# A hybrid scan kernel in which the SSD decay rows are loaded with repetition, head pairs share TensorE by column halves, and z is gated at its projection

## The chip, the cores and the metric

One core of one Trainium2 chip runs the whole program. The metric is the device time of one execution in microseconds. The engines are TensorE (PE in the rows), VectorE (DVE), ScalarE (ACT), GpSimd (POOL) and the queue processor SyncE (SP), which here only issues DMAs; ScalarE issues some too.

## The reference, cut to what matters

The model has two layers over 512 latent tokens and 256 context tokens (T = 768 columns in all), width 1024. The first layer runs a gated linear attention (GLA, 4 heads) and a Mamba-2 scan (SSD, 16 heads of 64 features, 2 groups with a state of 128) in both directions. The change is in the SSD part:

```python
dt = softplus(dt.reshape(b, l, 2, SSD_HEADS) + dt_bias)
log_a = dt * (-exp(a_log))
...
y, ss_f, ss_b = bidir_scan(ch, bh * dt[0], bh * dt[1], xh, log_a[0], log_a[1], init[2], init[3])
y = y + xh * d_skip
y = y.reshape(b, l, SSD_INNER) * silu(z)
y = rmsnorm(y.reshape(b, l, SSD_GROUPS, SSD_INNER // SSD_GROUPS), ssd_norm)
```

`bidir_scan` runs S_t = a_t S_(t-1) + k_t x_t, o_t = S_t q_t forwards and backwards. As matrices it is this: with g the running sum of log_a of a head, token s reaches token t by (B_s . C_t) dt_s exp(g_t - g_s), forwards for s <= t and backwards for s >= t, and the latent tokens also see the states at the end of the context. The rest of layer 1 (an mLSTM) and the two feed-forward blocks are not touched.

## The kernel before

**Layout.** Features lie on partitions, the 768 tokens are columns. Dense projections go unit by unit: a unit is 128 output features, its 8 weight blocks come through a ring of four, GpSimd splits them into a high and a low part (L600 to L603), and TensorE makes three products of each (L746, L820 for the mixed stage). `proj` in DRAM holds the 44 tiles of the input projection: x tiles from 32, z tiles from 24, B at 40 and 41, C at 42 and 43.

**Around the scan.** The mixed stage interleaves the units of g, z and x (table MIXED, L54) with the GLA heads; ScalarE evicts a unit's PSUM into `stage` (L1386). Then `out0` projects the GLA output to the residual (8 units, VectorE adds them at L2094). In its middle VectorE and ScalarE run the **row chain**: 32 rows, 16 heads in two directions. ScalarE loads `rowc` and `dcol` (L1487 to L1491), takes `r_ab` (L1494), VectorE softplus and the running sums `Grow` (L2122 to L2145) and `r_nb` (ln dt - g, L2148); TensorE turns `r_nb`, `r_al` into columns (L976, L979), copied to `nb` and `al` (L1516).

**The scan.** Eight pairs of heads. Per group of 8 heads `group_products` (L994 to L1001) makes B C of every chunk, `group_copies` (L1528) puts it into `cb` (six chunks of 128 tokens: four latent of 512 columns, two of context, 2560 columns) and B transposed into `Btok`. Per pair: TensorE transposes x (L1011), ScalarE copies it to `xtok` (L1532), VectorE weights it (`xal`, L2186), TensorE makes the context states (L1019), VectorE copies them (`ssS`, L2193). Per head:

- `rows` (L1030): TensorE spreads the head's row of g over 128 partitions by a one-hot product into PSUM, one slot of two banks for each direction.
- `exponents` (L2161): VectorE adds the column `nb` to the diagonal blocks; GpSimd sets the wrong side of them to -1e30 (L622, L626).
- `decays`: ScalarE takes the exponential of the strips off the diagonal straight from PSUM with `nb` as bias (L1549), of the first 512 columns into `Cb` (L1552), and of the masked diagonal blocks (L1556).
- `head_weights`: VectorE adds the backward diagonal blocks to the forward ones (L2171, L2173), multiplies all by `cb` into `Mm` (2560 columns, L2176), and C into `Cb` (L2178).
- `head_products`: four products of x with the weights (L1044), two of the states with `Cb` (L1046), two for the context (L1048), all into 64 of 128 partitions of one PSUM slot.

Then `output` adds D x (L2198) and multiplies by silu(z) (L2200), for which `gate_z` (L1560) loads its own table on ScalarE between two `decays`. x and z of a pair are loaded by ScalarE (L1503, L1504). At the end come squares, sums over features (L692), the spread of the norm (L698) and `out1`, the second output projection (L746).

**Order.** Each engine works its list in the order written and waits on counters; nothing is reordered. `Dm`, `Cb`, `xt`, `xtok`, `ssS` have two buffers.

## Time and profile before

| | |
|---|---|
| median of 3 runs | 2860.43 us (2858.86 to 2861.58) |
| profiled execution | 2862.67 us, span in the trace 2860.9 us |
| TensorE busy | 2559.3 us, 89% |
| VectorE busy | 1496.9 us, 52% |
| GpSimd busy | 1019.1 us, 36% |
| ScalarE busy | 644.4 us, 23% |
| granted TensorE clock, mean | 0.92 of full speed |
| the scan: end of `out0` to first product of `out1` | 676.8 to 993.7 us |

### The profile page before, as it was taken

How to read it: one execution, taken by the hardware profiler on the slowest of the kernel's cores; microseconds unless marked ns; L12 is line 12 of the kernel's file. 1: busy time of each engine (PE TensorE's matmuls, PEld its weight loads, DVE VectorE, ACT ScalarE, POOL GpSimd, SP SyncE). 2: the span in 40 equal slices, each digit the busy share in tenths (PEclk: the TensorE clock that was granted, in tenths of full speed). 3: DMA queues.
4: the chain of work that ended last, by engine and by line, in shares of the span. 5: the costliest groups of instructions: out<-in, count | busy, mean ns of one | idle time of the engine just before them, and what ended most of it. 6: DMA issues, size and time to landing. Idle time of an engine off the chain costs nothing.

```text
span 2860.9 us, 33680 instructions
## 1 busy us (share of the span) xinstructions
PE 2559.3 (89%) x12095; PEld 1946.5 (68%) x12095; DVE 1496.9 (52%) x2513; ACT 644.4 (23%) x984; POOL 1019.1 (36%) x806
## 2 busy tenths in 40 slices
PE   6999999968777799999999989699787796899998
PEld 2888888855333377888888878575444543788886
DVE  3685766654545535887788645520544345422223
ACT  3103444323444313100000032111222021210001
POOL 2443333322111042545434435333200310677663
PEclk9999999977777799999999989899888898999999
DMA  7753233421000021444434425445412210233331
GB/s 244 239 153 116 89 109 111 168 74 52 22 33 22 0 67 45 118 111 125 117 102 112 104 60 155 150 134 170 135 38 66 88 41 30 74 103 97 94 93 55
DMA packets 387698, 280.22 MB, mean 98 GB/s; under 512 B 31042, under 2 KB 350972, under 8 KB 387580
## 3 DMA queue, kind: packets, MB, share of 16 engines
q1 hardware_dynamic: 326876, 182.63, 22.2%
q10 hardware_dynamic: 60704, 96.00, 9.8%
q8 instruction: 76, 1.25, 0.2%
q14 instruction: 42, 0.34, 0.0%
HBM read 236.91 MB, written 41.68 MB: 97 GB/s over the span
## 4 chain that ended last, share of the span: by engine, by line
PE 80%; DVE 11%; ACT 5%; issue 2%; DMA 1%; ACTq 0%; SPq 0%; DVEq 0%; POOL 0%; POOLq 0%
PE PS L746 51%; PE PS L820 6%; PE PS L1222 3%; PE PS L1044 3%; PE PS L1030 2%; PE PS L1192 2%; PE PS L1129 1%; PE PS L910 1%; PE PS L677 1%; PE PS L1046 1%; PE PS L692 1%; ACT Dm L1549 1%; DVE Gn L1989 1%; PE PS L698 1%; PE PS L876 1%
## 5 line engine op out<-in xcount | busy, mean ns | idle before, releaser
L746 PE MATMUL PS<-act_hi,w_hi 128*128 128x512 f32 (+1 forms) x2080 | 639.1, 365 | 46.2 <-DVE act_lo L1911 18.1
L600 POOL TENSOR_TENSOR w_hi<-w_raw,ones 128x128 fp32r<-128x128 f32 x244 | 148.6, 609 | 1361.6 <-PE PS L746 855.2
L746 PE MATMUL PS<-act_lo,w_hi 128*128 128x512 f32 (+1 forms) x2080 | 623.9, 358 | 0.0
L746 PE MATMUL PS<-act_hi,w_lo 128*128 128x512 f32 (+1 forms) x2080 | 623.4, 357 | 0.0
L603 POOL TENSOR_TENSOR w_lo<-w_raw,w_hi 128x1024 fp32r<-128x1024 f32 (+1 forms) x244 | 594.8, 2438 | 20.4
L746 PEld LDWEIGHTS PS<-act_hi,w_hi 128*128 128x128 f32 x2080 | 345.1, 192 | 106.6 <-issue 44.0
L746 PEld LDWEIGHTS PS<-act_hi,w_lo 128*128 128x128 f32 x2080 | 344.3, 191 | 58.9
L746 PEld LDWEIGHTS PS<-act_lo,w_hi 128*128 128x128 f32 x2080 | 345.2, 191 | 57.5 <-issue 0.5
L1854 DVE SCALAR_TENSOR_TENSOR mf_acc<-mf_ring,cs,mf_acc 128x128 f32<-128x128 f32 x784 | 283.1, 436 | 2.0
L601 POOL TENSOR_SCALAR w_hi<-w_raw 128x896 fp32r<-128x896 f32 (+1 forms) x244 | 239.0, 979 | 0.0
L2094 DVE SCALAR_TENSOR_TENSOR xT<-PS,modv,xT 128x512 f32<-128x512 f32 (+1 forms) x120 | 74.9, 658 | 275.5 <-PE PS L746 274.8
L746 PE MATMUL PS<-hid_hi,w_hi 128*128 128x512 f32 (+1 forms) x528 | 164.5, 366 | 0.0
L746 PE MATMUL PS<-hid_hi,w_lo 128*128 128x512 f32 (+1 forms) x528 | 161.5, 360 | 0.0
L746 PE MATMUL PS<-hid_lo,w_hi 128*128 128x512 f32 (+1 forms) x528 | 161.5, 360 | 0.0
L2251 DVE TENSOR_TENSOR fhp<-fsg,PS 128x768 f32<-128x768 f32 (+1 forms) x44 | 36.1, 821 | 203.7 <-PE PS L746 181.9
L820 PE MATMUL PS<-act_hi,w_hi 128*128 128x512 f32 x448 | 123.1, 356 | 5.3 <-ACT stage L1386 5.2
L1608 ACT ACTIVATE fsg<-PS 128x768 f32<-128x768 f32 (+1 forms) x44 | 31.0, 705 | 427.8 <-PE PS L746 427.7
L1030 PE MATMUL PS<-Grow,ident 32*128 32x256 f32 (+1 forms) x128 | 75.3, 745 | 47.9 <-ACT Cb L1552 47.9
L2254 DVE TENSOR_TENSOR hid_lo<-fhp,hid_hi 128x512 f32 (+2 forms) x44 | 93.7, 2131 | 45.8 <-ACT hid_hi L1611 45.8
L820 PE MATMUL PS<-act_lo,w_hi 128*128 128x512 f32 x448 | 116.9, 342 | 0.0
L820 PE MATMUL PS<-act_hi,w_lo 128*128 128x512 f32 x448 | 116.9, 342 | 0.0
L1611 ACT ACTIVATE hid_hi<-fhp 128x768 f32 (+1 forms) x44 | 32.6, 740 | 306.0 <-DVE fhp L2251 306.0
(319 smaller groups left out, 3397.0 us busy)
## 6 DMA issues: line engine op xcount, KB each, us to landing
w_raw<-in_ffn_w SPq DMA_DIRECT2D x120, 512.0 KB, 4.0
mf_ring<-in_w_mod SPq DMA_DIRECT2D x56, 512.0 KB, 4.0
w_raw<-in_a_w_in SPq DMA_DIRECT2D x44, 512.0 KB, 5.5
proj<-stage ACTq DMA_DIRECT2D x44, 384.0 KB, 2.7
w_raw<-in_b_w_up SPq DMA_DIRECT2D x32, 512.0 KB, 4.0
m_ring<-in_w_mod SPq DMA_DIRECT2D x12, 1024.0 KB, 7.8
m_raw<-in_w_mod SPq DMA_DIRECT2D x4, 2048.0 KB, 17.2
w_raw<-in_a_w_out SPq DMA_DIRECT2D x16, 512.0 KB, 4.1
```

The lines of the kernel that those rows point to most:

```text
L600: pool.tensor_tensor(w_hi[:, s, 0], w_raw[:, s, 0], ones[:], ALU.mult)
L601: pool.tensor_scalar(w_hi[:, s, 1:kt], w_raw[:, s, 1:kt], 1.0, 1.0, ALU.mult, ALU.mult).then_inc(w_hi_done, 1)
L603: pool.tensor_tensor(w_lo[:, s, 0:kt], w_raw[:, s, 0:kt], w_hi[:, s, 0:kt].bitcast(F32), ALU.subtract).then_inc(w_split, 1)
L746: last = pe.matmul(slot(s)[:, c0:c1], w[:, s, k, :], x[:, k, c0:c1], start=k == 0 and w is w_hi and x is hi, stop=k == kt - 1 and w is w_lo)
L820: last = pe.matmul(slot((n + 1) % 2)[:, c0:c1], w[:, n % RING, k, :], x[:, k, c0:c1], start=k == 0 and w is w_hi and x is act_hi, stop=k = ...
L1030: last = pe.matmul(slot(d)[:, c0:c1], ident[0:32, r:r + 1].broadcast_to([32, P]), Grow[:, d, c0:c1], start=True, stop=True)
L1044: pe.matmul(y[:, 0:LAT], xtok[:, p % 2, c, f:f + 64], d[:, c * LAT:c * LAT + LAT], start=c == 0, stop=False)
L1192: last = pe.matmul(bank(SCORE_BANKS[i]), xch[:, t, c * P:c * P + P], qp[:, t], start=t == 0, stop=t == 3)
L1222: last = pe.matmul(bank(OUT_BANKS[t]), vt[:, c, t * P:t * P + P], Wf[:, c], start=i == 0, stop=i == 5)
L1854: ins = dve.scalar_tensor_tensor(acc, mf_ring[:, s % 2, k], c, acc, ALU.mult, ALU.add)
L2094: ins = dve.scalar_tensor_tensor(x, y, g, x, ALU.mult, ALU.add)
L2254: dve.tensor_tensor(lo, fhp[:, i, 0:n], hi.bitcast(F32), ALU.subtract).then_inc(hid_ready, 1)
```

## The change

1. **Loads of `rowc` and `dcol`** move from behind the last GLA head to the start of the mixed stage, on the same queue.
2. **Row transposes** (`r_nb`, `r_al`) are written between the sixth and the seventh unit of `out0` instead of after the eighth.
3. **z's silu** is taken when its unit is evicted from PSUM. In MIXED z comes two places ahead of an x, and one eviction per GLA head moves behind the output copies. The silu of z is loaded back into `yT` by SyncE, eight tiles in front of the scan.
4. **Rows** of g are written to DRAM (`g_d`) by SyncE, and come back repeated on 128 partitions, both directions of a head in one load of 128x2x768 (768 KB), two buffers. `rows` on TensorE is gone.
5. **Diagonal blocks.** GpSimd masks from `rows` into `Dm` and `Db` without waiting for VectorE; ScalarE adds `nb` as a bias while it takes the exponential; only four backward blocks get it from VectorE (`exponents`), in one instruction.
6. **Weights** are multiplied by `cb` in place, in four buffers `Dm`; `Mm` is gone.
7. **Pairs.** `pair_products` writes the products of the two heads of a pair alternately, the even head to partitions 0 to 63 of the output, the odd one to 64 to 127, states first. A pair's output slot alternates. `Cb` is one tensor with two heads.
8. **Order.** x tiles are loaded by SyncE behind the rows of the odd head and after the output of two pairs before, the second group's B and C ahead of time; ScalarE copies x between the two heads of a pair; the second group's products stand in the middle of pair 3.

The core of the diff:

```diff
 MIXED = [("z", 0)]
 for _h in range(GLA_HEADS):
-    MIXED += [("g", 2 * _h), ("g", 2 * _h + 1), ("z", 2 * _h + 1), ("x", 3 * _h), ("x", 3 * _h + 1), ("x", 3 * _h + 2)]
+    MIXED += [("g", 2 * _h), ("g", 2 * _h + 1), ("x", 3 * _h), ("z", 2 * _h + 1), ("x", 3 * _h + 1)]
     if _h < 3:
         MIXED += [("z", 2 * _h + 2)]
+    MIXED += [("x", 3 * _h + 2)]
 MIX0 = 16
 PROJ_TILE = {"g": G0, "z": Z0, "x": X0}
...
-        Mm = nc.alloc_sbuf_tensor_at("Mm", [P, 2, DB], F32, offset=act_hi_at)
...
+        cb = nc.alloc_sbuf_tensor_at("cb", [P, DM], F32, offset=act_hi_at)
+        Dm = [sb(f"Dm{i}", [P, DM], offset=4 * DM * i) for i in range(3)]
+        Dm.append(nc.alloc_sbuf_tensor_at("Dm3", [P, DM], F32, offset=act_hi_at + 4 * DM))
+        xal = nc.alloc_sbuf_tensor_at("xal", [P, 2, 2, 2, P], F32, offset=act_hi_at + 8 * DM)
+        Db = sb("Db", [P, 2, T], offset=30720)
+        rows = sb("rows", [P, 2, 2, T], offset=36864)
+        Cb = sb("Cb", [P, 2, 2, LAT], offset=49152)
...
+                    sp.wait_ge(r_grow, 4)
+                    for d in range(2):
+                        sp.dma_start(g_d[d], Grow[16 * d:16 * d + 16, d, :]).then_inc(g_out, 16)
...
+                    def load_rows(h):
+                        src = bass.AP(tensor=g_d.tensor, offset=g_d.offset + h * T, ap=[[0, P], [SSD_HEADS * T, 2], [1, T]])
+                        sp.dma_start(rows[:, h % 2], src).then_inc(rows_in[h % 2], 16)
...
+                    sp.wait_ge(mm_done, n0)
+                    for p in range(PAIRS):
+                        sp.dma_start(yT[:, p], proj0[Z0 + p]).then_inc(z_back, 16)
+                    sp.wait_ge(cb_mm, 6)
+                    sp.dma_start(bct[:, 0], proj0[B0 + 1]).then_inc(b1_in, 16)
+                    for h in range(2, SSD_HEADS):
+                        sp.wait_ge(exp_done, h - 1)
+                        load_rows(h)
+                        if h % 2 and h > 3:
+                            p = h // 2
+                            sp.wait_ge(y_done, p - 1)
+                            sp.dma_start(xt[:, p % 2], proj0[X0 + p]).then_inc(xt_in[p % 2], 16)
...
+                        D, row = Dm[h % 4], rows[:, h % 2]
+                        pool.wait_ge(rows_in[h % 2], ROWS_IN0 + 16 * (h // 2 + 1))
...
+                        if h >= 4:
+                            pool.wait_ge(y_mm, h // 2 - 1)
+                        for off, n, step, c0 in ((DL, 4, LAT + P, 0), (DC, 2, CTX + P, 4)):
+                            pool.affine_select(out=diagonals(D, off, n, step), in_=row[:, 0, c0 * P:(c0 + n) * P].rearrange("p (c t) -> p c t", t=P),
+                                               compare_op=ALU.is_ge, fill=-1e30, base=0, pattern=[[0, n], [1, P]],
+                                               channel_multiplier=-1).then_inc(mask_done, 1)
+                        if h >= 2:
+                            pool.wait_ge(fb_done, h - 1)
+                        pool.affine_select(out=diagonals(Db[:, h % 2], 0, 6, P), in_=row[:, 1].rearrange("p (c t) -> p c t", t=P),
+                                           compare_op=ALU.is_ge, fill=-1e30, base=0, pattern=[[0, 6], [-1, P]],
+                                           channel_multiplier=1).then_inc(mask_done, 1)
                     each_ring(pool, n0 + RING, count - RING, lambda r, s: split(r, s, kt))
...
+            project_unit("out0", n0 // RING + 1, 2, KD, act_hi, act_lo, T, act_ready, READY["gla"])
+            pe.wait_ge(ct_put, 2)
+            project_unit("out0", n0 // RING + 1, 3, KD, act_hi, act_lo, T, act_ready, READY["gla"])
...
-            def rows(h):
...
-            def head_products(h):
...
+            def pair_products(p):
+
+                y = slot(p % 2)
+                pe.wait_ge(cbeta_done, 2 * p + 2)
                 pe.wait_ge(ss_put, p + 1)
-                if p and h % 2 == 0:
-                    pe.wait_ge(y_put, p)
-                y, d = slot(2)[f:f + 64], Mm[:, h % 2]
+                if p >= 2:
+                    pe.wait_ge(y_put, p - 1)
+                for k in range(2):
+                    for f in range(2):
+                        last = pe.matmul(y[64 * f:64 * f + 64, 0:LAT], ssS[:, p % 2, k, 64 * f:64 * f + 64], Cb[:, f, k],
+                                         start=k == 0, stop=False)
+                last.then_inc(cb_read, 1)
+                if p == 3:
+                    group_products(1)
+                pe.wait_ge(m_done, 2 * p + 2)
                 for c in range(4):
-                    pe.matmul(y[:, 0:LAT], xtok[:, p % 2, c, f:f + 64], d[:, c * LAT:c * LAT + LAT], start=c == 0, stop=False)
-                for k in range(2):
-                    pe.matmul(y[:, 0:LAT], ssS[:, p % 2, k, f:f + 64], Cb[h % 2][:, k], start=False, stop=k == 1)
+                    for f in range(2):
+                        pe.matmul(y[64 * f:64 * f + 64, 0:LAT], xtok[:, p % 2, c, 64 * f:64 * f + 64],
+                                  Dm[(2 * p + f) % 4][:, c * LAT:c * LAT + LAT], start=False, stop=c == 3)
                 for c in range(2):
-                    last = pe.matmul(y[:, LAT:T], xtok[:, p % 2, 4 + c, f:f + 64], d[:, DC + c * CTX:DC + c * CTX + CTX],
-                                     start=c == 0, stop=c == 1)
+                    for f in range(2):
+                        last = pe.matmul(y[64 * f:64 * f + 64, LAT:T], xtok[:, p % 2, 4 + c, 64 * f:64 * f + 64],
+                                         Dm[(2 * p + f) % 4][:, DC + c * CTX:DC + c * CTX + CTX], start=c == 0, stop=c == 1)
                 last.then_inc(y_mm, 1)
...
+            x_transposes(1)
+            states(0)
+            for p in range(PAIRS):
+                pair_products(p)
+                if p + 1 < PAIRS:
+                    states(p + 1)
+                if p + 2 < PAIRS:
+                    x_transposes(p + 2)
...
+                src = a["a_ssd_D"][0]
+                act.dma_start(dcol[64 * f:64 * f + 64, :], bass.AP(tensor=src.tensor, offset=src.offset + f, ap=[[0, 64], [2, PAIRS]]),
+                              allow_slow_non_contiguous=True).then_inc(row_in, 16)
...
-                act.activation(stage[:, n % 2], slot((n + 1) % 2), ACT.Copy).then_inc(evac, 1)
+                act.activation(stage[:, n % 2], slot((n + 1) % 2), ACT.Silu if kind == "z" else ACT.Copy).then_inc(evac, 1)
...
-                evacuate(first + 4)
                 output_copy(h, 0)
...
                     output_copy(h, i)
+                evacuate(first + 4)
...
+                D, b, row = Dm[h % 4], Db[:, h % 2], rows[:, h % 2]
+                act.wait_ge(rows_in[h % 2], ROWS_IN0 + 16 * (h // 2 + 1))
...
+                    act.wait_ge(cb_read, CB_READ0 + h // 2)
+                act.activation(Cb[:, h % 2], row[:, :, 0:LAT], ACT.Exp).then_inc(cb_exp, 1)
+                if h >= 4:
+                    act.wait_ge(y_mm, h // 2 - 1)
+                for c in range(6):
+                    lo, hi, off = (0, 4, DL + c * LAT) if c < 4 else (4, 6, DC + (c - 4) * CTX)
+                    if c + 1 < hi:
+                        act.activation(D[:, off + (c + 1 - lo) * P:off + (hi - lo) * P], row[:, 0, (c + 1) * P:hi * P], ACT.Exp,
+                                       bias=nb[:, 0, c, h:h + 1])
+                    if c > lo:
+                        act.activation(D[:, off:off + (c - lo) * P], row[:, 1, lo * P:c * P], ACT.Exp, bias=nb[:, 1, c, 16 + h:17 + h])
+                act.wait_ge(mask_done, 3 * h + 2)
+                for c in range(6):
+                    at = DL + c * (LAT + P) if c < 4 else DC + (c - 4) * (CTX + P)
+                    act.activation(D[:, at:at + P], D[:, at:at + P], ACT.Exp, bias=nb[:, 0, c, h:h + 1])
                 act.wait_ge(mask_done, 3 * h + 3)
...
-                    act.activation(blocks, blocks, ACT.Exp).then_inc(exp_done, 1)
-
-            def gate_z(p):
-                act.wait_ge(xt_in, 32 * (p + 1))
-                act.activation(sz[:, p % 2], sz[:, p % 2], ACT.Silu).then_inc(z_silu, 1)
+                for c in (4, 5):
+                    act.activation(b[:, c * P:c * P + P], b[:, c * P:c * P + P], ACT.Exp, bias=nb[:, 1, c, 16 + h:17 + h])
+                act.wait_ge(e_done, h + 1)
+                act.activation(b[:, 0:LAT], b[:, 0:LAT], ACT.Exp).then_inc(exp_done, 1)
...
+            decays(0)
...
+            for p in range(2, PAIRS):
+                decays(2 * p)
+                x_copies(p)
+                if p == 4:
                     group_copies(1)
...
+                b = diagonals(Db[:, h % 2], 0, 4, P)
+                dve.wait_ge(mask_done, 3 * h + 3)
+                dve.tensor_tensor(b, b, nb[:, 1, 0:4, 16 + h:17 + h].broadcast_to([P, 4, P]), ALU.add).then_inc(e_done, 1)
...
+                dve.tensor_tensor(c, c, C.unsqueeze(1).broadcast_to([P, 2, LAT]), ALU.mult).then_inc(cbeta_done, 1)
+                dve.wait_ge(exp_done, h + 1)
+                f, x = diagonals(D, DL, 4, LAT + P), diagonals(b, 0, 4, P)
+                dve.tensor_tensor(f, f, x, ALU.add).then_inc(dve_own, 1)
+                f, x = diagonals(D, DC, 2, CTX + P), diagonals(b, 4 * P, 2, P)
+                chain.n[dve_own] += 1
+                chain(dve.tensor_tensor(f, f, x, ALU.add), fb_done)
+                dve.wait_ge(dve_own, chain.n[dve_own])
+                if h + 1 < SSD_HEADS:
+                    exponents(h + 1)
                 dve.wait_ge(cb_put, 6 * (h // 8) + 6)
...
+                dve.tensor_tensor(D[:], D[:], cb[:], ALU.mult).then_inc(m_done, 1)
...
+                chain(dve.scalar_tensor_tensor(xt[:, p % 2], xt[:, p % 2], dcol[:, p:p + 1], slot(p % 2), ALU.mult, ALU.add), y_put)
+                dve.wait_ge(z_back, Z_BACK0 + 16 * PAIRS)
+                chain(dve.tensor_tensor(yT[:, p], yT[:, p], xt[:, p % 2], ALU.mult), y_done)
...
+            for p in range(PAIRS):
+                head_weights(2 * p)
+                if p == 0:
+                    weighted_x(0)
+                else:
+                    state_copy(p)
+                    output(p - 1)
+                head_weights(2 * p + 1)
+                if p == 0:
+                    state_copy(0)
+                if p + 1 < PAIRS:
+                    weighted_x(p + 1)
```

TensorE through one pair of heads, before: the order of its list.

```order
L1011 MATMUL PS<-ident,xt 128x128 [waits ssd_ss_put,ssd_xt_in]
L1011 MATMUL PS<-ident,xt 128x128 x5
L1030 MATMUL PS<-Grow,ident 128x512 [waits ssd_rows_read]
L1030 MATMUL PS<-Grow,ident 128x256
L1030 MATMUL PS<-Grow,ident 128x512 [waits ssd_rows_read]
L1030 MATMUL PS<-Grow,ident 128x256
L1019 MATMUL PS<-xal,Btok 128x256 [waits ssd_xt_put,ssd_xal_done]
L1019 MATMUL PS<-xal,Btok 128x256
L1044 MATMUL PS<-Mm,xtok 64x512 [waits ssd_ss_put,ssd_xt_put,ssd_y_put,ssd_cbeta_done,ssd_m_done]
L1044 MATMUL PS<-Mm,xtok 64x512 x3
L1046 MATMUL PS<-Cb_114,ssS 64x512 x2
```

The transposes of the next x come first, then the four spread rows of a later head, then the states of this pair, and the products of one head into one half.

TensorE through one pair after the change (`Dm_103` and `Dm_104` are the weights of the even and the odd head):

```order
L1075 MATMUL PS<-xal,Btok 128x256 [waits ssd_ss_put,ssd_cb_put,ssd_xal_done]
L1075 MATMUL PS<-xal,Btok 128x256
L1065 MATMUL PS<-ident,xt 128x128 [waits ssd_xt_put,ssd_xt_in0]
L1065 MATMUL PS<-ident,xt 128x128 x5
L1088 MATMUL PS<-Cb,ssS 64x512 [waits ssd_ss_put,ssd_cbeta_done]
L1088 MATMUL PS<-Cb,ssS 64x512 x3
L1096 MATMUL PS<-Dm_103,xtok 64x512 [waits ssd_m_done]
L1096 MATMUL PS<-Dm_104,xtok 64x512
L1096 MATMUL PS<-Dm_103,xtok 64x512
L1096 MATMUL PS<-Dm_104,xtok 64x512
```

The spread rows are gone; the states and the transposes stand ahead of the pair's products, and these alternate between the two heads.

ScalarE before, from the last exponential of an odd head to the next head (`Cb_115` is one of its two C buffers):

```order
L1556 ACTIVATE Dm<-Dm 128x768
L1532 ACTIVATE xtok<-PS 128x768 [waits ssd_xt_tr]
L1560 ACT_TABLE_LOAD
L1560 ACTIVATE sz<-sz 128x768 [waits ssd_xt_in]
L1549 ACT_TABLE_LOAD [waits ssd_e_done]
L1549 ACTIVATE Dm<-PS,nb 128x384 [waits ssd_m_done]
L1549 ACTIVATE Dm<-PS,nb 128x256
L1549 ACTIVATE Dm<-PS,nb 128x128 x2
L1552 ACTIVATE Cb_115<-PS 128x512 [waits ssd_y_mm]
L1549 ACTIVATE Dm<-PS,nb 128x128 [waits ssd_e_done]
```

ScalarE after the change, the end of an even head, the copy of x and the start of the odd one. `x_put` counts the products that have read `Cb`, `mod_in2` the loads of an odd head's rows:

```order
L1579 ACTIVATE Dm_103<-rows,nb 128x128
L1582 ACTIVATE Dm_103<-rows,nb 128x128
L1586 ACTIVATE Dm_103<-Dm_103,nb 128x128 [waits ssd_mask_done]
L1586 ACTIVATE Dm_103<-Dm_103,nb 128x128 x5
L1589 ACTIVATE Db<-Db,nb 128x128 [waits ssd_mask_done]
L1589 ACTIVATE Db<-Db,nb 128x128
L1591 ACTIVATE Db<-Db 128x512 [waits ssd_e_done]
L1566 ACTIVATE xtok<-PS 128x768 [waits ssd_xt_tr]
L1573 ACTIVATE Cb<-rows 128x1024 [waits x_put,mod_in2]
L1579 ACTIVATE Dm_104<-rows,nb 128x384 [waits ssd_y_mm]
```

The table loads are gone from the scan; the copy of x stands between two heads, and each head now waits first for products that read `Cb` and then for `ssd_y_mm`, the products of two pairs before.

SyncE after the change, behind the first four weight loads of `out1`; before, it had only weight loads here:

```order
L588 DMA yT<-proj 128x768 [waits mm_done]
L588 DMA yT<-proj 128x768 x7
L590 DMA bct<-proj 128x768 [waits ssd_cb_mm]
L580 DMA rows<-g_d 128x2x768 [waits ssd_exp_done] x4
L597 DMA xt<-proj 128x768 [waits ssd_y_done]
L580 DMA rows<-g_d 128x2x768 [waits ssd_exp_done] x2
L597 DMA xt<-proj 128x768 [waits ssd_y_done]
L580 DMA rows<-g_d 128x2x768 [waits ssd_exp_done] x2
```

The eight loads of z wait for the end of `out0`, the second B for the first group's products; each load of rows waits for a head's exponentials, and a load of x stands behind the rows of an odd head.

## Rows read from the trace of the kernel before

**Rows 1.** Windows: us, busy PE, PEld, DVE, ACT, POOL; PEclk, DMA share, GB/s.

```profile
692.00:970.00 278.00, 216.73 (x458) 85.36 (x457) 137.44 (x149) 124.35 (x248) 32.14 (x48) 0.74 0.07 23
```

**Rows 2.** Timelines of ScalarE, VectorE, TensorE before 640 us; windows of two units.

```profile
620.97 0.94 ACT L1494 ACTIVATE r_ab<-dtT,rowc 32x768 f32<-32x768 f32 x1 [14.39 <-DMA dcol<-in_a_ssd_D]
...
639.13 2.19 DVE L2094 SCALAR_TENSOR_TENSOR xT<-PS,modv,xT 128x512 f32<-128x512 f32 x4
...
640.38 0.98 PE L746 MATMUL PS<-act_hi,w_hi 128*128 128x512 f32 x2 [14.46 <-issue]
...
640.30:651.40 11.10, 11.02 (x49) 9.51 (x50) 10.75 (x15) 2.84 (x4) 0.00 (x0) 0.77 0.01 1
651.40:659.90 8.50, 8.50 (x50) 7.37 (x49) 2.18 (x6) 0.30 (x1) 3.77 (x3) 1.00 0.21 62
```

**Rows 3.** TensorE's waits, 240 to 600 us: who, for whom, us, times, longest.

```profile
PE PS L820 <- ACT stage L1386: 5.2, 3, 2.1
```

**Rows 4.** The chain that ended last, through one pair of heads: start, us, what.

```profile
767.36 1.28 ACT L1560
...
772.81 5.48 PE PS L1030 x8
...
786.77 1.72 PE PS L1046 x4
...
804.60 1.28 ACT L1560
```

**Rows 5.** Timeline of TensorE, where head 6 gives way to head 7.

```profile
825.72 0.38 PE L1048 MATMUL PS<-Mm,xtok 128*64 128x256 f32 x1
825.73 0.64 PE L1044 MATMUL PS<-Mm,xtok 128*64 128x512 f32 x1
```

**Rows 6.** Timeline of ScalarE through one pair: copy of x, strips, C rows.

```profile
766.53 0.81 ACT L1532 ACTIVATE xtok<-PS 128x768 f32<-128x768 f32 x1 [10.34 <-PE PS L1011]
...
771.64 0.37 ACT L1549 ACTIVATE Dm<-PS,nb 128x128 f32<-128x128 f32 x1
...
771.89 0.38 ACT L1549 ACTIVATE Dm<-PS,nb 128x128 f32<-128x128 f32 x1
...
789.89 1.46 ACT L1549 ACTIVATE Dm<-PS,nb 128x128 f32<-128x128 f32 x4
791.20 0.62 ACT L1552 ACTIVATE Cb<-PS 128x512 f32<-128x512 f32 x1
```

**Rows 7.** Two windows of one pair, then VectorE's timeline and GpSimd's.

```profile
767.30:770.10 2.80, 0.00 (x0) 0.00 (x0) 2.64 (x4) 2.75 (x4) 0.00 (x0) 1.00 0.00 0
780.30:785.90 5.60, 4.88 (x7) 1.50 (x8) 5.41 (x5) 0.00 (x0) 0.00 (x0) 0.55 0.00 0
...
781.39 0.43 DVE L2173 TENSOR_TENSOR Dm<-Dm 128x256 f32<-128x256 f32 x1
...
796.19 0.96 DVE L2173 TENSOR_TENSOR Dm<-Dm 128x256 f32<-128x256 f32 x1
...
795.70 1.18 POOL L626 TENSOR_SCALAR_AFFINE_SELECT Dm<-Dm 128x768 f32<-128x768 f32 x1 [1.84 <-DVE Dm L2161]
```

**Rows 8.** Timeline of TensorE from the first output projection to the second.

```profile
676.26 0.51 PE L746 MATMUL PS<-act_hi,w_lo 128*128 128x512 f32 x2
...
680.23 6.71 PE L994 MATMUL PS<-bct 128*128 128x512 f32 x8 [1.04 <-ACT al L1517]
...
765.62 0.88 PE L1011 MATMUL PS<-ident,xt 128*128 128x128 f32 x6
...
982.43 5.28 PE L692 MATMUL PS<-ones,snacc 128*128 128x1 f32 x24 [9.16 <-DVEq L2224]
...
993.72 0.59 PE L746 MATMUL PS<-act_hi,w_hi 128*128 128x512 f32 x2 [0.68 <-DVE act_lo L2234]
```

**Rows 9.** DMA issues: what, queue, count, KB each, median us to landing.

```profile
xt<-proj ACTq DMA_DIRECT2D x8, 384.0 KB, 3.1
```

**Rows 10.** Costliest groups: count | busy, mean ns | idle before, releaser.

```profile
L603 POOL TENSOR_TENSOR w_lo<-w_raw,w_hi 128x1024 fp32r<-128x1024 f32 (+1 forms) x244 | 594.8, 2438 | 20.4
```

254 lines of the change are left out of this document (87 added, 167 removed).

## The prediction, made before the changed kernel ran

> **What bounds the kernel now.** I read the chain of work that ended last, then the busy times by stretch, then the timelines of the engines in one stretch. The dense projections are a bound that the change leaves alone: TensorE runs them back to back. The SSD head scan is another matter. From the end of the first output projection (676.8 us) to the first product of the second (993.7) there are 317 us [rows 8], and in the long middle of it TensorE is busy 217 of 278 us at a granted clock of 0.74, VectorE 137, ScalarE 124 [rows 1]. Nobody is full, and TensorE is busy mostly because it is slow. The chain through one pair of heads goes from one to the other [rows 4]: a table load for the silu of z (767.36), the spread rows on TensorE (5.48 us, after a pause), the products of the even head, among them 1.72 us with the states, ScalarE again, the odd head, and at 804.60 the same table load: 37.2 us for a pair, eight times. The second thing to see lies ahead of it: TensorE stands for 14.46 us until 640.38, because VectorE reaches the residual tiles whose PSUM it needs only at 639.13: it is in the row chain, whose first step, on ScalarE at 620.97, waited 14.39 us for the small loads of dcol and rowc [rows 2].
>
> **Part by part, outside the scan.**
> (a) The loads of rowc and dcol go from behind the GLA heads to the start of the mixed projections, 380 us earlier. Of its 14.39 us of wait ScalarE's first row step keeps about 0.5 (the queue's turn), so the whole row chain moves 13.9 us up, and with it the residual tiles, from 639.1 to 625.3. TensorE then waits about 0.5 us instead of 14.46. Cover: the two units before the pause, which end at 626; if the chain came later, the wait would be back one for one. Also the unit after the pause took 11.1 us at a granted clock of 0.77 where the next took 8.5 at 1.00 [rows 2]: 2.5 us more. The row transposes, some 1.4 us out of the 3.4 that lie between the end of the projection and the B C products at 680.23 [rows 8], move in between two of its units; with the row chain earlier, their input is there before. Sum: 14.0 + 2.5 - 1.4, the first output projection ends 15.1 us earlier.
> (b) Order of the mixed units and silu of z at its eviction. Three times TensorE waited for an eviction that stood behind a convolution on VectorE, 5.2 us in all [rows 3]; the tile two places ahead is now a z tile, whose buffer is free early. I take the 5.2 us off (bounds 0 and 5.2). z's silu costs two more table loads (1.28 us) on a ScalarE that is under half busy there: nothing, and the two per pair in the scan go.
> So the scan starts at 656.5 instead of 676.8: **20.3 us**.
>
> **The scan, part by part.** Call X the end of the copy of the transposed x of pair p-1 on ScalarE. The rows that TensorE spread now come by DMA (768 KB a head), the head weights are multiplied in place, the 24 products of a pair are written as alternating column halves.
> ScalarE, one head: exponentials of two times 512 columns (0.62 us long, of which some 0.14 lie under the next: 0.96), eight strips (two times the 1.31 from 789.89 to 791.20), eight diagonal blocks with a bias (0.25 from start to start, 771.64 to 771.89: 2.0), the 512 of the backward blocks (0.62), and hops: **6.5 us** [rows 6]. The copy of x takes 0.81.
> VectorE from X [rows 7]: the weights of x, the output and its product with z, 2.64 us in the first window; state copy, two adds, the large product and C times decay, 5.41 in the second; a bias add of 512 columns, 0.7 from the adds beside it; with hops **9.4 us**. In the same time ScalarE does head 2p-1 (6.5).
> Now the order matters. SP issues the load of x for pair p behind the rows of head 2p+1 and only after that output (the buffer is the same): it lands 3.1 us later [rows 9], at X+12.6 (9.4, 3.1 and a hop). TensorE has its transposes of pair p ahead of pair p-1's state products: 0.88 us at the full level [rows 8], 1.1 here, X+13.7. Then four state products: eight pieces of 0.43 at the full level (1.72 us for four pieces of one head [rows 4]). Two halves side by side are shown once, at 825.7, where head 6's last pieces go to one half and head 7's first to the other: a 512-column piece of 0.64 us starts within 0.01 us of a 256-column one of 0.38 [rows 5]. The same at like sizes makes four slots, at the lower level (after a pause of 10 us) 0.86 each: 3.5, X+17.2. ScalarE's head 2p waits for that, since they free the buffer of C: 6.5 us, then the copy of x 0.81: **X+24.6**. The large products of the pair (8.6 us at the lower level) and the next states lie beside that, ending at X+27, needed at the next X+7. The row loads are twice the load of x (768 KB against 384 in 3.1 us), so between 3.1 and 6.2 us; I take 5 [rows 9]. They are issued 12 us or more before their strips need them: hidden.
> VectorE and GpSimd: where GpSimd's select lay beside VectorE's 256-column add, the add took 0.96 instead of 0.43 [rows 7]. The selects no longer wait for VectorE and may meet any of its operations. One head's steps lie in the chain above; its selects take at most 1.18 us for each direction by that row, so the bounds per pair are 0 and 2.4, and I take 0.5. **A pair: 25.1 us instead of 37.2.**
> The Trainium skill (SBUF — State Buffer, Who interferes with whom) has this as an exclusive lock: a VectorE operation with two SBUF inputs and a GpSimd operation that reads SBUF don't run together, the later one waits in full. By that the adds and selects, now all from SBUF, would pay up to the whole select each time, which is the upper bound of the sentence before; the trace's longer add agrees in kind.
>
> **Start and end of the scan**, from its start T0. GpSimd's last weight split, some 4 us with its longest part 2.44 [rows 10], comes before the masks (1.0), the diagonal blocks (2.0) and the last 512 columns: first head's exponentials done at T0+7.7, second at 14.2. Only then ScalarE copies the B C products, which TensorE can't go on without (two banks); they took 6.71 us for the first four [rows 8], so 7.0 in all: 21.2. Large product of head 0, head 1 (rows of head 2 land at 27, since SP waits for the B C products), state copy at 33, state products 36.5, heads 2 and 3 on ScalarE 49.6, x of pair 2 lands 53.6, products 58.3, head 4 and copy: X of pair 2 at **T0+66**. Five more pairs of 25.1 are 125.5; the second group's B C products, with copies between, hold the large products of pair 3 back: **8 us** (bounds 3 and 10). After the last X: head 15, its product at 14.9, large products until 23.6, output, square, add: **28**. Then the norm, 11.3 us from its first sums (982.43) to 993.72 as before [rows 8]. T0+238.8 against 316.9: **78 us**.
>
> **The sum.** 20.3 + 78 = 98; for hops of SP and the two loads that share the queues I take 2 back: 96. The profiled execution took 2862.7 (span 2860.9), 2.2 above the median of the runs, 2860.4; the difference applies to either, so **2765**. 0.2% (6 us) is about what a measurement of this kernel can tell from no change.
>
> **The rivals.**
> - *TensorE at the full level in the scan* (0.10). For: it is busy 15 of 25 us. Against: the pause of 10 us comes just before the critical pieces, and after a pause of 6 us the spread rows took 5.48 us for eight pieces at 772.81 [rows 4]. Transposes and state products lose 1.9 us per pair, start 4: 2765 - 5x1.9 - 4 = 2751.
> - *The selects block in full* (0.10), which is what the skill's lock rule (same page and section) would make of them: 1.9 us more per pair, six pairs: 2776.
> - *Repeating loads are slow* (0.07): all 128 partitions read the same 3 KB rows of HBM, which no row of the trace does. x of pair p lies behind such a load in SP's queue. At 12 us instead of 5 it lands 7 us later, seven times: 2814.
> - *The same, and slower than before* (0.04): at 19 us a load the gain is gone (7x14 = 98); at 22, 36 GB/s, 2765 + 7x17 = 2884.
> - The forecast: 0.58. Within 0.2%: 0.01.
>
> **How the numbers follow.** The likeliest case is 2765, its own range 2752 to 2783 (group 3 to 10, selects 0 to 2.4, mixed stage 0 to 5.2). With the full level below and the serial halves above, 2745 to 2800 leaves out the slow loads and some tail. Faster 0.95, same 0.01, slower 0.04.
>
> **What would show it.** Right: TensorE's pause at 626 gone; no table loads between 660 and 890; copies of x on ScalarE about 25 us apart, with ScalarE idle some 10 us before each even head, waiting for TensorE; state products starting in twos at 0.86; the x loads landing just ahead of the transposes. Wrong: row loads over 10 us; state products one after another; ScalarE busy without a gap (then a head costs more than 6.5 us); a pair near 20 us, if the wait on x is not where I put it; or a stall in the mixed stage behind a z eviction.

## The result and the profile after

The changed kernel takes 2781.96 us (median, 2777.15 to 2786.14) against 2861.01 for the kernel before in the same comparison: ratio 0.972, 95% interval 0.970 to 0.974. The prediction said 2765, 2745 to 2800. The sign, the size and most places of the scan are right. Of the forecast gain of 96 us, 17 are missing. By the places in the table, 14.7 us are missing ahead of the scan and 3.6 in it; behind it 1.1 came on top, where the forecast had taken 2 off.

| us, profiled executions | before | after | gain | forecast gain |
|---|---|---|---|---|
| first product of `out0` | 579.4 | 575.0 | 4.4 | 5.2 |
| end of `out0` | 676.8 | 671.1 | 5.6 | 20.3 |
| first product of `out1` | 993.7 | 913.6 | 80.1 | 98 |
| scan between the last two | 316.9 | 242.5 | 74.4 | 78 |
| span | 2860.9 | 2779.7 | 81.2 | 96 |

Two windows of the changed kernel (columns as in rows 1): the unit of `out0` behind TensorE's pause, then the whole scan.

```profile
633.20:644.30 11.10, 11.09 (x49) 9.59 (x50) 10.75 (x15) 4.18 (x5) 0.00 (x0) 0.75 0.14 37
671.14:913.64 242.50, 112.88 (x398) 50.03 (x396) 128.81 (x136) 127.04 (x312) 52.39 (x51) 0.68 0.27 79
```

They answer to [rows 2] and [rows 1]. In the whole scan TensorE is busy 113 us (243 before), at a mean granted clock of 0.68, and ScalarE 127 of 242. The unit behind the pause still takes 11.1 us, at 0.75. TensorE's waits between 240 and 700 us (columns as in rows 3):

```profile
PE PS L796 <- issue: 8.0, 1, 8.0
...
PE PS L870 <- ACT stage L1438: 0.6, 1, 0.6
```

The evictions that cost 5.2 us [rows 3] now cost 0.6. But the pause before the fifth unit, forecast at 0.5 us, is 8.0. The row chain, timelines of ScalarE, VectorE and TensorE:

```profile
606.42 0.94 ACT L1540 ACTIVATE r_ab<-dtT,rowc 32x768 f32<-32x768 f32 x1 [0.49 <-ACT stage L1445]
...
620.22 11.71 DVE L2156 SCALAR_TENSOR_TENSOR r_p<-r_p,r_s 32x768 f32<-32x768 f32 x7
631.96 2.19 DVE L2120 SCALAR_TENSOR_TENSOR xT<-PS,modv,xT 128x512 f32<-128x512 f32 x4
...
633.21 0.98 PE L796 MATMUL PS<-act_hi,w_hi 128*128 128x512 f32 x2 [8.01 <-issue]
```

ScalarE's first step is at 606.42, as forecast (its wait fell from 14.39 to 0.49 us, [rows 2]). The residual tiles were forecast for 625.3 and come at 631.96: on the way seven row steps take 11.71 us. The view of that line in the changed kernel gives their shortest, median and longest duration in ns. Behind it stand the two parts of GpSimd's weight splits that lie beside the first and the last of the seven:

```profile
L2156 DVE SCALAR_TENSOR_TENSOR r_p<-r_p,r_s x7: 945/1093/3033, 620.2 to 629.0; 32x768 f32<-32x768 f32 x7
...
619.86 2.58 POOL L646 TENSOR_TENSOR w_lo<-w_raw,w_hi 128x1024 fp32r<-128x1024 f32 x1
...
628.20 2.92 POOL L646 TENSOR_TENSOR w_lo<-w_raw,w_hi 128x1024 fp32r<-128x1024 f32 x1
```

Now one pair of the scan. First VectorE's weights of x, then its C weights of the odd head behind the output; the issue of the load of x; TensorE's transposes, state products and large products; ScalarE's heads 4 and 6 and the copies of x between the heads:

```profile
741.46 0.76 DVE L2212 TENSOR_TENSOR xal<-xtok,al 128x256 f32<-128x256 f32 x2 [13.15 <-ACT xtok L1566]
...
750.27 1.23 DVE L2193 TENSOR_TENSOR Cb<-Cb,bct 128x1024 f32<-128x1024 f32 x1
...
750.26 0.34 SPq L597 DMA_DIRECT2D xt<-proj  x1
...
754.97 1.54 PE L1065 MATMUL PS<-ident,xt 128*128 128x128 f32 x6 [10.62 <-DMA xt<-proj]
756.44 2.81 PE L1088 MATMUL PS<-Cb,ssS 128*64 128x512 f32 x8
759.09 3.60 PE L1096 MATMUL PS<-Dm,xtok 128*64 128x512 f32 x16
...
733.85 1.06 ACT L1573 ACTIVATE Cb<-rows 128x1024 f32<-128x1024 f32 x1 [11.80 <-PE PS L1088]
...
740.64 0.79 ACT L1566 ACTIVATE xtok<-PS 128x768 f32<-128x768 f32 x1
...
759.36 1.06 ACT L1573 ACTIVATE Cb<-rows 128x1024 f32<-128x1024 f32 x1 [11.15 <-PE PS L1088]
...
766.15 0.79 ACT L1566 ACTIVATE xtok<-PS 128x768 f32<-128x768 f32 x1
```

The order is the one written down. The copy of x ends at X = 741.43. The C weights of the odd head start at 750.27, when the output is done and the load of x is issued (X+8.8; forecast 9.4). The load lands 4.7 us later (forecast 3.1), the transposes take 1.54 (1.1), the state products 2.8 to 3.7 (3.5), ScalarE waits for them and is at its next copy of x 25.5 us after the last (25.1). Two kinds of load share SyncE's queue (KB, median us to landing). The rows are near their estimate of 5; the loads of x, half the size, take as long, though they took 3.1 on ScalarE's queue [rows 9]:

```profile
rows<-g_d SPq DMA_DIRECT2D x16, 768.0 KB, 5.4
...
xt<-proj SPq DMA_DIRECT2D x8, 384.0 KB, 5.3
```

How long a load of x takes goes with its distance to the rows in front of it. In the scan it lands 6.1 us after its issue when it is issued 0.4 to 0.6 us behind a load of rows, and 4.3 to 5.4 when it is 2.0 us behind. In ve_order and all_edits (below) it is issued 3.6 us or more behind the rows, mostly when they have landed, and takes 2.9 to 3.4.

### The profile page after: what moved, and what is told of

Same layout as the page of the kernel before. It is cut to its first block, busy times and chain, and to the rows that moved or that the text cites. A ratio compares the mean times of both kernels' runs of the same rounds, so it can differ in the third digit from the quotient of the medians.

```text
span 2779.7 us, 33411 instructions
## 1 busy us (share of the span) xinstructions
PE 2432.3 (88%) x11967; PEld 1897.7 (68%) x11967; DVE 1472.5 (53%) x2481; ACT 641.1 (23%) x1042; POOL 1040.0 (37%) x806
## 4 chain that ended last, share of the span: by engine, by line
PE 57%; DVE 7%; ACT 2%; issue 1%; DMA 1%; DVEq 0%; ACTq 0%
PE PS L796 45%; PE PS L1268 3%; PE PS L1238 2%; PE PS L1175 2%; PE PS L1201 1%; PE PS L742 1%; PE PS L748 1%; PE PS L1214 1%; PE PS L805 1%; DVE xcr L1978 0%; DVE mf_acc L1880 0%; DVE mtmp L2422 0%; PE PS L1250 0%; DMA xmr<-xm_d 0%; DVE nacc L1912 0%
## 5 line engine op out<-in xcount | busy, mean ns | idle before, releaser
L1880 DVE SCALAR_TENSOR_TENSOR mf_acc<-mf_ring,cs,mf_acc 128x128 f32<-128x128 f32 x784 | 276.2, 426 | 2.0
L2283 DVE TENSOR_TENSOR hid_lo<-fhp,hid_hi 128x512 f32 (+2 forms) x44 | 85.9, 1953 | 45.8 <-ACT hid_hi L1637 45.8
L796 PEld LDWEIGHTS PS<-hid_lo,w_hi 128*128 128x128 f32 x528 | 87.9, 190 | 16.6
```

Of the source, the lines that this page charges most:

```text
L796: last = pe.matmul(slot(s)[:, c0:c1], w[:, s, k, :], x[:, k, c0:c1], start=k == 0 and w is w_hi and x is hi, stop=k == kt - 1 and w is w_lo)
L1880: ins = dve.scalar_tensor_tensor(acc, mf_ring[:, s % 2, k], c, acc, ALU.mult, ALU.add)
L2283: dve.tensor_tensor(lo, fhp[:, i, 0:n], hi.bitcast(F32), ALU.subtract).then_inc(hid_ready, 1)
```

## Experiments

Ends of stages of every kernel, from its profiled execution:

| kernel | first `out0` | end `out0` | first `out1` | scan | span |
|---|---|---|---|---|---|
| before | 579.4 | 676.8 | 993.7 | 316.9 | 2860.9 |
| after | 575.0 | 671.1 | 913.6 | 242.5 | 2779.7 |
| a_loads | 577.4 | 669.2 | 989.9 | 320.7 | 2850.2 |
| mixed_only | 572.9 | 669.4 | 990.2 | 320.9 | 2860.9 |
| res_first | 576.1 | 661.8 | 905.3 | 243.5 | 2778.6 |
| splits_wait | 575.7 | 665.0 | 904.9 | 240.0 | 2774.9 |
| halves_serial | 576.4 | 666.4 | 908.9 | 242.5 | 2776.2 |
| one_half | 575.7 | 671.1 | 930.6 | 259.5 | 2793.8 |
| states_first | 574.5 | 669.5 | 879.6 | 210.1 | 2741.0 |
| ve_order | 574.6 | 665.2 | 851.6 | 186.4 | 2719.7 |
| early_masks | 576.2 | 666.7 | 895.1 | 228.4 | 2764.5 |
| all_edits | 576.9 | 665.5 | 839.7 | 174.2 | 2710.4 |

What stands behind the scan is the same 8056 matmuls in all of them, and it takes from 1860 us (a_loads) to 1873 (res_first). One profiled span is therefore no measure for a few us; the stages are a better one.

### The loads alone (a_loads)

In the kernel before, the six lines that load `rowc` and `dcol` move up, and these two tiles to free addresses:

```diff
             act.dma_start(rd_raw[:, :, 64:128], win[:, :, COL_DT - 32:COL_DT + 32]).then_inc(rd_in, 16)
+            act.dma_start(rowc[:, 0:1], a["a_ssd_dt_bias"][0].rearrange("d (h o) -> (d h) o", o=1)).then_inc(row_in, 16)
...
             act.wait_ge(o_mm, 24)
-            act.dma_start(rowc[:, 0:1], a["a_ssd_dt_bias"][0].rearrange("d (h o) -> (d h) o", o=1)).then_inc(row_in, 16)
```

> The kernel before with one edit: the loads of rowc and dcol at the start of the mixed stage. The prediction: the residual tiles come 13.9 us earlier, TensorE's pause of 14.5 us shrinks to 0.5 and the unit behind it runs at the full clock, so 15 to 17 us less than before. Theory A, formed from the trace after (seven row steps 11.71 us instead of 6.82, one of them 3.03 us instead of 0.95): the row chain now lies beside GpSimd's weight splits and is made longer by them, the pause stays 7 to 8 us, the unit behind it stays slow, and the gain is 6.5 to 8 us. If the slower chain comes from something else in the changed kernel (its silu or its new order ahead), the seven steps take 6.8 us here and the gain is 14 or more.

Ratio to before 0.9977 (0.9959 to 0.9995), 2856.0 us. VectorE's timeline and TensorE's wait:

```profile
620.56 11.71 DVE L2130 SCALAR_TENSOR_TENSOR r_p<-r_p,r_s 32x768 f32<-32x768 f32 x7
...
PE PS L746 <- issue: 7.6, 1, 7.6
```

And the row of the same steps in the kernel before, which the prediction didn't show:

```profile
632.27 6.82 DVE L2130 SCALAR_TENSOR_TENSOR r_p<-r_p,r_s 32x768 f32<-32x768 f32 x7
```

The seven steps take 11.71 us here too, in a kernel with nothing else of the change in it, and the pause is 7.6 instead of 14.5: theory A. The end of `out0` comes 7.6 us earlier. The pause gives 6.8 of them; `out0` also started 2.0 earlier in this execution, and its first four units took 2.0 longer.

### GpSimd kept away from the row chain (splits_wait)

```diff
+                if name == "out0":
+                    each_ring(pool, n0, RING, lambda r, s: split(r, s, kt))
+                    split(n0 // RING + 1, 0, kt)
+                    pool.wait_ge(evac, n0 + 2)
+                    for s in (1, 2, 3):
+                        split(n0 // RING + 1, s, kt)
+                    continue
```

> The changed kernel in which GpSimd waits, behind the split for the fifth unit of the first output projection, until VectorE has added the first two residual tiles; only then it splits the weights of units six to eight. Theory A (VectorE's row steps are held up by GpSimd beside them): the seven row steps take 6.8 us instead of 11.7, TensorE's pause falls from 8.0 to about 3, 4 to 6 us less than the changed kernel. The rival, that the row steps are slow for a reason of their own: they stay at 11 to 12 us, the pause stays at 8, and the time is 2782 or more by what the later splits cost.

Ratio 0.9713 (0.9697 to 0.973), 2778.8 us. The same rows as above:

```profile
615.09 6.83 DVE L2163 SCALAR_TENSOR_TENSOR r_p<-r_p,r_s 32x768 f32<-32x768 f32 x7
621.95 2.19 DVE L2127 SCALAR_TENSOR_TENSOR xT<-PS,modv,xT 128x512 f32<-128x512 f32 x4
...
PE PS L803 <- issue: 2.1, 1, 2.1
```

The same seven steps on the same data take 6.83 us, to 0.01 us what they took in the kernel before, and the pause is 2.1. The edit moved only GpSimd's splits, so it was they that made the steps long. The later steps of the chain, beside which the splits now lie, become long instead (the scans of 3.88 us take 6.71). TensorE therefore waits 2.1 us at the row transposes, and the unit behind them becomes a slow one, 10.9 us. Little is won: 3.2 us on the medians, where 4 to 6 were expected.

### The residual ahead of the chain (res_first)

```diff
             chain(dve.tensor_scalar(r_p[:], r_e[:], 2.0, None, ALU.add))
+            dve.wait_ge(x_rl, 16)
+            residual("out0", 0, 2, T, tiles=(0, 1))
             chain(dve.reciprocal(r_p[:], r_p[:]))
...
-            dve.wait_ge(x_rl, 16)
-            residual("out0", 0, 2, T, tiles=(0, 1))
```

> The changed kernel with the first two residual tiles of the first output projection written ahead of the reciprocal in VectorE's row chain, where VectorE stands idle for 3.9 us, instead of behind the seven row steps. If VectorE's place in its list is the cause of TensorE's pause of 8.0 us, the pause is gone; the row chain ends as before, so the row transposes, reached 10 us earlier, wait 2 to 3 us: 7 to 9 us less than the changed kernel, 2773 to 2775. If the weight split of the next unit or another input is behind it, the pause stays and the time is that of the changed kernel, 2782.

Ratio 0.970 (0.9684 to 0.9716), 2776.9 us. VectorE's first residual tiles, the seven steps, and TensorE's one wait at the row transposes:

```profile
607.88 2.19 DVE L2120 SCALAR_TENSOR_TENSOR xT<-PS,modv,xT 128x512 f32<-128x512 f32 x4
...
619.38 9.71 DVE L2158 SCALAR_TENSOR_TENSOR r_p<-r_p,r_s 32x768 f32<-32x768 f32 x7
...
PE PS L1026 <- DVE xT L2120: 2.0, 1, 2.0
```

The pause is gone, and with it the slow unit behind it. But TensorE now waits 2.0 us at the transposes, as expected, and the unit behind them becomes the slow one, 11.0 us. `out0` ends at 661.8, 9.3 us earlier than in the changed kernel. Some 4.8 of these are a shorter first stretch of the stage, which belongs to the execution (see under mixed_only); the edit itself is worth about 5, and the medians differ by 5.0, where 7 to 9 were expected. So the pause needs two things: a chain that is late, and VectorE's list, which has the tiles behind it.

### The order of the mixed units alone (mixed_only)

```diff
-    MIXED += [("g", 2 * _h), ("g", 2 * _h + 1), ("z", 2 * _h + 1), ("x", 3 * _h), ("x", 3 * _h + 1), ("x", 3 * _h + 2)]
+    MIXED += [("g", 2 * _h), ("g", 2 * _h + 1), ("x", 3 * _h), ("z", 2 * _h + 1), ("x", 3 * _h + 1)]
     if _h < 3:
         MIXED += [("z", 2 * _h + 2)]
+    MIXED += [("x", 3 * _h + 2)]
```

(and `evacuate(first + 4)` behind the output copies, on the kernel before)

> The kernel before with only the new order of the g, z and x units and the later eviction in each GLA head; z is gated in the scan as before. The prediction: TensorE's three waits for evictions go, 5.2 us less. Theory B, from the trace after (the stage ends 4.4 us earlier, but the stretch behind its next pause runs at the lower clock for 12.3 us instead of 5.5 and gives back 3.7): the stage ends 4.4 us earlier here too, and how much is left depends on how long the lower clock lasts after that pause: 0.7 to 4.4 us. If it is the order that costs something later, the loss shows here as a wait of TensorE and not as a lower clock.

Ratio 0.9987 (0.9971 to 1.0004): not to be told from no change as a whole. By stages it is: `out0` starts at 572.9, 6.5 us earlier than before (4.4 were expected), and ends 7.4 earlier, with no new wait of TensorE; in this execution 3.9 us go again in the scan and 3.5 behind it, in stages whose code is that of before. TensorE's three waits were at the third unit of the second, third and fourth head. That unit needs the eviction of the head's first g tile, and the buffer for it held the x tile two places ahead, which is a z tile now: z stands two places ahead of a g, not of an x. The term of 5.2 us was right in its place (the kernels with that order start `out0` 2.5 to 6.5 us earlier than before) and is under the noise of the whole.

The changed kernel lost 3.7 of its 4.4 us again before the pause. TensorE's sums of squares there, and a window of the stretch, in the changed kernel:

```profile
579.01 2.55 PE L742 MATMUL PS<-ones,gm 128*128 128x1 f32 x12
...
575.03:588.50 13.47, 13.47 (x48) 11.88 (x49) 2.74 (x4) 6.17 (x8) 0.00 (x0) 0.53 0.21 68
```

and in ve_order, whose code up to here is the same:

```profile
578.17 1.39 PE L742 MATMUL PS<-ones,gm 128*128 128x1 f32 x12
...
574.60:588.00 13.40, 10.52 (x52) 8.62 (x52) 5.51 (x7) 6.97 (x9) 0.00 (x0) 0.88 0.20 68
```

Both stood still for 4.9 us before it. One is at the lower level (1.2 GHz) for 12 us, the other for 3, then at 2.4. From the first product of `out0` to the end of the fourth unit it is 45.0 to 45.5 us in five of the kernels that have TensorE's list of the change up to here (ve_order, early_masks, splits_wait, halves_serial, res_first), 48.3 in all_edits and 49.7 to 50.2 in three (the changed kernel, states_first, one_half). So the edits don't decide how long that stretch is; each kernel was profiled in one execution, and what decides it stays open.

### The order of the products (halves_serial)

```diff
-                for c in range(4):
-                    for f in range(2):
+                for f in range(2):
+                    for c in range(4):
```

(the same for the state products and the context)

> The changed kernel with the 24 products of a pair in another order: all of a kind of the even head, then those of the odd head, instead of alternating; the number and the operands are the same. If alternating halves run side by side, as the prediction took it and eight state pieces in 3.68 us suggest, the state products go from 3.5 to about 7 us per pair, on the path, and the large ones from 5 or 6 to 10 or more, beside it except in the last pair: the scan takes 25 to 32 us more (267 to 275 instead of 242.5). If TensorE runs them one after another either way, the scan stays at 242 to 244.

Ratio 0.971 (0.9686 to 0.9735), 2778.6 us; the scan is 242.5, to 0.1 us that of the changed kernel, where 25 to 32 us more were expected. TensorE's timeline for one pair, the states, then the large products:

```profile
751.33 3.02 PE L1088 MATMUL PS<-Cb,ssS 128*64 128x512 f32 x8
754.18 4.08 PE L1096 MATMUL PS<-Dm,xtok 128*64 128x512 f32 x13
757.67 0.65 PE L1100 MATMUL PS<-Dm,xtok 128*64 128x256 f32 x2
758.10 0.59 PE L1096 MATMUL PS<-Dm,xtok 128*64 128x512 f32 x1
...
759.38 1.03 PE L1100 MATMUL PS<-Dm,xtok 128*64 128x256 f32 x4
```

The eight state pieces take 3.0 us although written head by head: TensorE starts the odd head's while the even head's run. Of the large ones thirteen start within the first 3.5 us, though the even head has only eight of that kind. But the first four start alone, 0.43 us apart; in all eight pairs the odd head's first product starts together with the third of the even head's four. Each half then works through its own list: the even head's context pieces (L1100, 757.67) start while three of the odd head's large ones (the last at 758.95), written ahead of them, have not. With the context the large products take 6.2 us instead of 4.5 in this pair and lie beside ScalarE's work, so the scan doesn't show it. The scan came out as the second branch of the expectation has it, but not for its reason, that products run one after another. The rival of the prediction, that the halves don't run side by side, is out. For two products a head the alternation isn't needed; for six it saves 1.7 us in this pair, and only in the last pair does anything wait for them.

### Both heads in one half (one_half)

```diff
-                        last = pe.matmul(y[64 * f:64 * f + 64, 0:LAT], ssS[:, p % 2, k, 64 * f:64 * f + 64], Cb[:, f, k],
-                                         start=k == 0, stop=False)
+                        last = pe.matmul(y[0:64, 0:LAT], ssS[:, p % 2, k, 64 * f:64 * f + 64], Cb[:, f, k],
+                                         start=k == 0 and f == 0, stop=False)
```

(the same for the other products of a pair)

> The changed kernel with all 24 products of a pair written to partitions 0 to 63, those of the odd head too, so that TensorE can't run the two heads in different column halves; the output is therefore not the reference's (the two heads are summed in one half, the other is left), while counts, sizes, waits and order are the same. If the two halves at once are what keeps the state products short (pairs of pieces that start within 0.01 us of each other, in the alternating order and in the other one), these go from 2.8 to 3.7 us to 5.5 to 7.4 per pair and the products of the last pair from 5.7 to 11: the scan takes 25 to 35 us more than 242.5. If the halves are worth nothing, the scan stays at 242.

Ratio 0.9774 (0.9759 to 0.9789), 2800.1 us; the scan is 259.5. The kernel leaves out the odd head's half of the output. The same rows:

```profile
759.28 5.04 PE L1088 MATMUL PS<-Cb,ssS 128*64 128x512 f32 x8
764.16 7.03 PE L1096 MATMUL PS<-Dm,xtok 128*64 128x512 f32 x16
771.02 1.89 PE L1100 MATMUL PS<-Dm,xtok 128*64 128x256 f32 x8
```

Two halves at once are worth 17 us of scan, less than the 25 to 35 expected. The state products go from 2.8 to 3.7 us to 4.7 to 6.2 and not to 7, since TensorE reaches the full level in their course: in the pair shown the first piece takes 1.11 us and the last 0.59. The pairs without the second group go from 25.5 to 27.0 us to 27.2 to 29.5.

### What the critical loop is (states_first, ve_order)

states_first changes the place of the transposes on TensorE:

```diff
                 last.then_inc(cb_read, 1)
+                if p and p + 1 < PAIRS:
+                    x_transposes(p + 1)
...
-                if p + 2 < PAIRS:
-                    x_transposes(p + 2)
```

> The changed kernel with one order changed on TensorE: the transposes of the next pair's x stand behind the state products of a pair instead of ahead of them. If the load of x and its transposes are on the path, as the prediction has it (state products at 756.44 although their C weights are done at 751.5), these no longer wait for them: 5 us less for each pair, pairs of 20 to 21 us instead of 25.5 to 27, the scan 212 to 220 instead of 242.5. If something else ends last there (the rows of the next head, the buffers of the weights, VectorE), a pair stays over 23 us and the scan over 230.

Ratio 0.9601 (0.9575 to 0.9626), 2746.6 us, scan 210.1. TensorE and ScalarE in one pair:

```profile
743.26 3.68 PE L1088 MATMUL PS<-Cb,ssS 128*64 128x512 f32 x8 [8.14 <-DVE Cb L2193]
...
732.35 0.79 ACT L1566 ACTIVATE xtok<-PS 128x768 f32<-128x768 f32 x1
...
747.05 1.06 ACT L1573 ACTIVATE Cb<-rows 128x1024 f32<-128x1024 f32 x1 [7.13 <-PE PS L1088]
...
753.85 0.80 ACT L1566 ACTIVATE xtok<-PS 128x768 f32<-128x768 f32 x1
```

The state products wait for the C weights and no longer for the load; a pair takes 21.5 us. The scan is 2 us below the expected range of 212 to 220. The load of x and its transposes stood in the loop, as the prediction has it: one order on one engine, with no work less, takes 32 us off the scan.

ve_order adds this on VectorE (`head_weights` split in three):

```diff
+                c_weights(2 * p)
+                add_blocks(2 * p)
+                if p != 1:
+                    weighted_x(p)
+                c_weights(2 * p + 1)
+                state_copy(p)
+                times_cb(2 * p)
+                if p:
+                    output(p - 1)
+                add_blocks(2 * p + 1)
+                times_cb(2 * p + 1)
```

> The kernel of the run before, and on VectorE the odd head's C weights and the copy of the states go ahead of the even head's large product. The state products then start some 4 us behind the copy of x instead of 10, while ScalarE is still at the odd head. If the path is the one that the prediction wrote down, ScalarE is the bound after it: two heads of 7.0 us and the copy of x 0.8, so pairs of 15 to 17 us and a scan of 185 to 200. If the loads of the rows (5.4 us, two buffers, and the load of x in the same queue) are behind it, a pair is 18 to 20 us and the scan 205 to 215.

Ratio 0.9527 (0.9505 to 0.9549), 2725.7 us, scan 186.4. TensorE and ScalarE:

```profile
717.52 5.36 PE L1098 MATMUL PS<-Dm,xtok 128*64 128x512 f32 x16 [0.44 <-DVE Dm L2211]
722.72 1.03 PE L1102 MATMUL PS<-Dm,xtok 128*64 128x256 f32 x8
723.68 1.13 PE L1075 MATMUL PS<-xal,Btok 128*128 128x256 f32 x4
725.38 1.94 PE L1088 MATMUL PS<-Cb,ssS 128*64 128x512 f32 x8 [0.56 <-issue]
...
717.12 0.81 ACT L1566 ACTIVATE xtok<-PS 128x768 f32<-128x768 f32 x1 [0.96 <-PE PS L1065]
...
727.41 1.06 ACT L1573 ACTIVATE Cb<-rows 128x1024 f32<-128x1024 f32 x1 [2.71 <-PE PS L1088]
...
734.90 0.81 ACT L1566 ACTIVATE xtok<-PS 128x768 f32<-128x768 f32 x1 [0.60 <-PE PS L1065]
```

The scan is in the expected range of 185 to 200, but what comes next was expected wrong: a pair takes 17 to 20 us (17.8 here), and ScalarE still waits 2.7 for state products. By this timeline these stand behind the large products of the pair before, which wait for VectorE until 717.52, and behind the states (723.68): an engine's list again, and not ScalarE's work or the rows. No run changed that order, so this reading is not tested.

### The start of the scan (early_masks)

```diff
-                    each_ring(pool, n0, RING, lambda r, s: split(r, s, kt))
-
                     for h in range(SSD_HEADS):
+                        if h == 2:
+                            each_ring(pool, n0, RING, lambda r, s: split(r, s, kt))
```

(and on VectorE the first two `exponents` ahead of the last residual tile, on SyncE the rows of heads 2 and 3 ahead of the second B)

> The changed kernel with GpSimd's masks of the first two heads ahead of the four weight splits of the second output projection, VectorE's bias adds for them ahead of its last residual tile, and the rows of heads 2 and 3 loaded without waiting for the first group's products. In the changed kernel ScalarE waits 17.1 us for the first mask and copies the first B C products only 14.5 us behind the end of the first output projection. If that start is on the path as the prediction has it, the copies begin there at once and the scan is 13 to 16 us shorter (226 to 230 instead of 242.5). If the loads of z or of the rows hold the first pair instead, less than 5 us.

Ratio 0.9662 (0.9634 to 0.969), 2767.3 us, scan 228.4: 14.1 less. In the changed kernel ScalarE stands for 17.09 us before its first masked blocks, and copies B C at 685.70:

```profile
676.05 1.86 ACT L1586 ACTIVATE Dm<-Dm,nb 128x128 f32<-128x128 f32 x6 [17.09 <-POOL Dm L670]
...
685.70 1.06 ACT L1562 ACTIVATE cb<-PS 128x512 f32<-128x512 f32 x2
```

Three edits go together here, and which of them is worth what was not separated. In early_masks the copies begin 0.9 us behind the end of `out0`:

```profile
667.68 0.60 ACT L1563 ACTIVATE cb<-PS 128x512 f32<-128x512 f32 x1 [0.18 <-PE PS L1049]
```

### All four edits (all_edits)

> The changed kernel with the edits of four earlier runs together: the first two residual tiles ahead of the row chain, the masks of the first two heads ahead of the weight splits, the transposes of x behind the state products, and VectorE's new order. If the parts add up, the first output projection ends at 660 to 663, the scan takes 170 to 175 us (186.4 with the new orders, less 14 at its start), and the whole is 2700 to 2712. If the earlier masks only shift a wait (rows of heads 2 and 3, the copies of the first group), the scan stays at 180 to 186 and the whole at 2712 to 2720.

Ratio to before 0.9454 (0.944 to 0.9469), 2710.6 us. That is 71 us less than the changed kernel on the medians, which come from two comparisons, and 76 by their ratios. The scan (columns as in rows 1):

```profile
665.47:839.66 174.19, 108.37 (x397) 47.70 (x396) 138.86 (x134) 119.26 (x287) 46.53 (x48) 0.77 0.36 110
```

174.2 us, as the parts add up. `out0` ends at 665.5 rather than by 663; its first four units took 48.3 us, some 3 more than in the kernels with the short stretch.

## Why the prediction was right, and where it wasn't

- **The scan: right, 74.4 us for 78.** The loop (VectorE, load of x, transposes, state products, ScalarE) was forecast at 25.1 and is 25.5 to 27. Within it the load of x was 1.6 us too cheap in the pair shown and the transposes 0.4, and VectorE was 0.6 too dear. The load is long where rows are still in flight in its queue: behind landed rows it takes 3 us. The second group costs 7.3 us more than a pair (forecast 8). X of pair 2 is at T0+70.3 (66), and 3.0 of these 4.3 us are the load of x again, which takes 6.1 us there. The tail from the last X to the norm is 23.5 (28). So the mechanism is right, but that the sum is within 4 us owes something to luck: start and pairs together are 8.2 us too short, the tail 4.5 too long. states_first shows that the load and the transposes stood in the loop.
- **The row loads: right.** 5.4 us for 768 KB (estimate 5), all partitions reading the same rows. Both rivals on slow loads are out. What was missed is what they do to the load of x behind them.
- **The silu of z: right.** No table load on ScalarE between its row steps and the squares.
- **Term (a): wrong by 10 us**, the step "the whole row chain moves 13.9 us up". Its start moved 14.5 up, but its length did not stay: in the kernel before GpSimd stood still beside the seven steps, and 12 us earlier its weight splits are in the way. The seven steps take 11.71 instead of 6.82 us, and earlier ones are longer too (L2150 with 2.26 for 0.55). The pause fell by 6.5 us instead of 14.0, and since a pause stayed, so did the slow unit behind it (2.5). a_loads and splits_wait show that the splits did it, res_first that VectorE's list carried it to TensorE. The prediction weighed this effect, but only in the scan, for the selects, where it took 0.5 us a pair. There it costs VectorE little, since GpSimd is the one that waits: a select of four blocks takes up to 2.7 us beside VectorE's large product (L2204) and 0.63 alone, and the product keeps its 2.82. From the third pair on, only the product with z (L2226) is longer, 1.19 for 0.96 in four of them. The Trainium skill's lock rule (SBUF — State Buffer, Who interferes with whom) says that a VectorE instruction with two SBUF inputs and a GpSimd instruction that reads SBUF exclude each other, and whichever comes second waits for the whole of the first. The trace agrees here: the first of the seven started at 620.22, when a part of a split was at work until 622.44, and took 3.03 us where it takes 0.95 alone, 2.1 more for 2.2 us of that part. Between the splits, from 623.3 to 626.2, three steps took 0.95 each. By that rule term (a) was to be had from the trace of before: from 607 to 630 four splits of some 4 us stand on GpSimd, where VectorE would now run its chain.
- **Term (b): its place right, its size hidden.** 4.4 of 5.2 us came. 3.7 of them were lost again in the profiled execution, where the stretch at the lower clock was long; five other kernels with the same list there have a short one, two a long one, and one lies between.
- **The halves: right.** Four slots for eight pieces, 2.8 to 3.7 us for 3.5; one_half shows that the two halves give them. The alternating order, to which the prediction tied them, isn't needed for these eight.
- **The full level all through the scan** didn't occur, as forecast: the transposes at 754.97 take 1.54 us against 0.88 at the full level, the clock of the scan is 0.68. But the level can change within the state products: in the pair shown its first pieces take 1.12 us and its last 0.59, which is why that pair has 2.8 us and others up to 3.7.

## What to carry to other kernels

Moving a chain earlier moves it beside other work: before you carry its length over, look at what the other engines and the loads in the same queue do in its new place, above all GpSimd beside two-input steps of VectorE. When a pause is to go, ask first whether the waiting work stands behind unrelated work in an engine's list; the four edits that gained some 70 us here only changed the order of such lists. And ask where the pause goes: two edits that shortened it brought half of it or more back at the next wait. For differences under 0.5% of such a kernel compare stages and not spans, since identical code behind them varied by 13 us, and compare each stage with other kernels that share its code, since one of them varied by 5 us.

## What the runs showed of the hardware

- **TensorE's halves run side by side without being written so, up to a point.** Alternating, two pieces of different halves start within 0.01 us of each other. Written head by head, eight state pieces take about 3 us just the same. Of the large products the odd head's first starts with the even head's third, so thirteen pieces start from 754.18 to 757.67, where one half alone would have started nine. Each half keeps its own order, and a product of one half can start ahead of products of the other that are written before it. All eight pairs of halves_serial show the same. Longer lists were not tried.
- **A load behind another in one queue pays while that one is in flight.** 384 KB landed in 6.1 us when issued 0.4 to 0.6 us behind 768 KB, in 4.3 to 5.4 at 2.0 us, and in 2.9 to 3.4 when issued 3.6 us or more behind (the changed kernel, ve_order and all_edits).
- **VectorE and GpSimd: whoever comes second waits.** A two-input step of VectorE went from 0.95 to 3.03 us behind a part of a weight split that was at work, and GpSimd's select from 0.63 to as much as 2.7 behind a VectorE product that kept its 2.82.
- **The lower clock after equal pauses lasts differently.** After 4.89 and 4.90 us of pause the same products ran at the lower level for 12 and for 3 us, 13.5 against 9.1 us from the first product to the spread of the norm at 588.50 and 583.67. What decides it was not tried.
- **Repeated reads of the same rows are not slow.** 768 KB for 128 partitions from 6 KB of DRAM land in a median of 5.4 us, some 145 GB/s into SBUF.
